# Diagonal and finest-level scores of the recurrence heads, taken as channel sums in rounded products

## The reference, cut to what matters

```
b = jnp.cumsum(gi, axis=-2)
diff = b[..., :, None, :] - b[..., None, :, :]
decay = jnp.exp(jnp.where(causal, diff, -jnp.inf))
scores = jnp.einsum('bhtk,bhsk,bhtsk->bhts', qi, ki, decay)
o = jnp.einsum('bhts,bhsv->bhtv', scores, vi) + ...
```

## Time and profile before

| what | value |
|---|---|
| median of 3 runs | 1628.47 us |
| the profiled execution, its own time | 1628.97 us |
| its span | 1627.2 us |
| PE busy | 1620.3 us, 100% |
| DVE busy | 1109.9 us, 68% |
| ACT busy | 842.2 us, 52% |
| POOL busy | 181.7 us, 11% |
| a stream slab, from issue to landing (median) | 4.7 us |

### The profile page before, as it was taken

How to read it: one execution, slowest core, us unless ns; L and a number is a source line. 1 busy time by engine, 2 the same in 40 slices (tenths; PEclk the granted TensorE clock), 3 DMA queues, 4 the chain that set the end, 5 groups by cost and what they waited for, 6 DMA issues and landing times.

```text
span 1627.2 us, 35049 instructions
## 1 busy us (share of the span) xinstructions
PE 1620.3 (100%) x13332; PEld 1615.8 (99%) x13332; DVE 1109.9 (68%) x1917; ACT 842.2 (52%) x1192; POOL 181.7 (11%) x166
## 2 busy tenths in 40 slices
PE   9999999999999999999999999999999999999999
PEld 9999999999999999999999999999999999999999
DVE  7548767888888876655986665566555665555774
ACT  7575765666666665433654334443444334443452
POOL 3101000111111100055300000000000000035200
PEclk9999999999999999999999999999999999999999
DMA  9577895565555467755675865588557775555564
GB/s 274 161 230 225 267 270 174 164 191 162 192 166 181 155 206 229 270 181 185 173 214 186 247 207 180 188 259 243 174 181 242 245 222 185 181 197 181 167 192 144
DMA packets 151178, 329.17 MB, mean 202 GB/s; under 512 B 16944, under 2 KB 79536, under 8 KB 150608
## 3 DMA queue, kind: packets, MB, share of 16 engines
q1 hardware_dynamic: 143888, 326.00, 64.3%
q10 hardware_dynamic: 7232, 2.43, 0.6%
HBM read 310.08 MB, written 18.30 MB: 202 GB/s over the span
## 4 chain that ended last, share of the span: by engine, by line
PE 98%; DMA 1%; DVE 1%; ACT 0%; SPq 0%; issue 0%
PE bank L380 29%; PE bank L381 29%; PE bank L382 28%; PE bank L398 3%; PE bank L400 3%; PE bank L403 2%; PE bank L768 1%; DMA raw<-in_stream 1%; PE bank L795 0%; PE bank L787 0%; PE bank L766 0%; PE bank L788 0%; PE bank L757 0%; PE bank L732 0%; PE bank L770 0%; PE bank L778 0%
## 5 line engine op out<-in xcount | busy, mean ns | idle before, releaser
L355 ACT CAST whi<-raw 128x1024 fp32r<-128x1024 f32 x532 | 547.9, 1048 | 470.7 <-PE bank L382 388.5
L380 PE MATMUL bank<-a_hi,whi 128*128 128x264 f32 x2576 | 734.2, 285 | 0.1
L381 PE MATMUL bank<-a_hi,wlo 128*128 128x264 f32 x2576 | 729.7, 283 | 0.0
L382 PE MATMUL bank<-a_lo,whi 128*128 128x264 f32 x2576 | 729.4, 283 | 0.0
L360 DVE TENSOR_TENSOR wlo<-raw,whi 128x1024 fp32r<-128x1024 f32 x518 | 629.6, 1246 | 109.8 <-ACT whi L355 108.8
L380 PEld LDWEIGHTS bank<-a_hi,whi 128*128 128x128 f32 x2576 | 485.2, 188 | 0.8 <-issue 0.7
L381 PEld LDWEIGHTS bank<-a_hi,wlo 128*128 128x128 f32 x2576 | 485.5, 188 | 0.1
L382 PEld LDWEIGHTS bank<-a_lo,whi 128*128 128x128 f32 x2576 | 482.9, 187 | 0.0
L380 PE MATMUL bank<-b_hi,whi 128*128 128x264 f32 x1280 | 363.1, 284 | 0.0
L381 PE MATMUL bank<-b_hi,wlo 128*128 128x264 f32 x1280 | 362.6, 283 | 0.0
L382 PE MATMUL bank<-b_lo,whi 128*128 128x264 f32 x1280 | 362.4, 283 | 0.0
(11 more groups left out here) (222 smaller groups left out, 1497.7 us busy)
## 6 DMA issues: line engine op xcount, KB each, us to landing
raw<-in_stream SPq DMA_DIRECT2D x532, 512.0 KB, 4.7
m_spill<-stage SPq DMA_DIRECT2D x32, 132.0 KB, 3.7
lev<-m_spill SPq DMA_DIRECT2D x16, 264.0 KB, 2.8
room<-in_x SPq DMA_DIRECT2D x7, 528.0 KB, 7.8
S<-in_state_hgrn SPq DMA_DIRECT2D x6, 512.0 KB, 6.7
out_new_hgrn_sample<-S SPq DMA_DIRECT2D x6, 512.0 KB, 6.8
S<-in_state_gla SPq DMA_DIRECT2D x5, 512.0 KB, 6.7
out_new_gla_sample<-S SPq DMA_DIRECT2D x5, 512.0 KB, 7.5
```

Of the source, the lines that this page charges most:

```text
L355: act.copy(whi[:, s, :], raw[:, s, :]).then_inc(hi_ready, 1)
L380: pe.matmul(out, whi[:, s, w], hi[:, k0 + k, :], start=start and k == 0, stop=False)
L381: pe.matmul(out, wlo[:, s, w], hi[:, k0 + k, :], start=False, stop=False)
L382: mm = pe.matmul(out, whi[:, s, w], lo[:, k0 + k, :], start=False, stop=stop and k == HT - 1)
```

## The change

- Queries times keys of each token (the diagonal) are multiplied channel by channel on POOL (`dots_of`), the two factors of level 7 on DVE (`dots`, columns 0 to 127). ACT rounds these 384 columns (`dots_hi`), DVE makes their rest (`dots_lo`), and PE sums them over the channels by two rounded products with `ones_r` (`sum_dots`), placed behind `turn_kd` and ahead of slab 5. The two diagonal products and the product of level 7 go.
- ACT makes `turned` ahead of `slab(6)` instead of behind it, then waits for the products and rounds them. DVE waits for that rounding behind `slab(4)`.
- DVE's `slab(6)` moves from ahead of the masking to behind the seven additions. Level 7 is masked by an instruction of its own (128 columns), and the second mask instruction has two levels instead of three.
- `ident` is loaded by three transfers of 128 x 128 in another order of blocks, and the order of the blocks in `pairs` turns with it; the constants' semaphore counts 8 instead of 6.

```diff
@@ -183,0 +184,3 @@
+    with nc.sbuf_tensor("dots", [P, 3 * P], F32) as dots, nc.sbuf_tensor("dots_hi", [P, 3 * P], F32R) as dots_hi, \
+         nc.sbuf_tensor("dots_lo", [P, 3 * P], F32R) as dots_lo:
+        pass
@@ -250 +253 @@
-        "act": ["v_tok_ready", "lev_exp", "kd_exp", "kd_tok_ready", "sq_ready", "sq_rounded",
+        "act": ["v_tok_ready", "lev_exp", "kd_exp", "kd_tok_ready", "sq_ready", "parts_rounded",
@@ -252 +255 @@
-        "dve": ["sq_parted", "lev_sub", "lev_ready", "kd_ready", "masked", "probs_ready", "sg_ls",
+        "dve": ["parts_ready", "lev_sub", "lev_ready", "kd_ready", "masked", "probs_ready", "sg_ls",
@@ -308,0 +312,12 @@
+    def dots_now(H, D):
+        return 2 * H + 2 if D == 1 else H + (HH + 2)
+    def first_now(H):
+        return 2 * H + 2
+    def second_now(H):
+        return 2 * H + 3
@@ -318,0 +334,5 @@
+    def turned_blocks(dots):
+        ap = dots[:, 2 * P:3 * P]
+        return bass.AP(ap.tensor, ap.offset, [list(ap.ap[0]), [-P, 2], [1, P]])
@@ -486,2 +506 @@
-        for dst, name in ((masks, "masks"), (ident, "ident"), (head_gain, "head_gain"),
-                          (gate_b, "gate_b")):
+        for dst, name in ((masks, "masks"), (head_gain, "head_gain"), (gate_b, "gate_b")):
@@ -488,0 +508,2 @@
+        for to, of in ((0, 0), (1, 2), (2, 1)):
+            sp.dma_start(ident[:, to * P:(to + 1) * P], t["ident"][:, of * P:(of + 1) * P]).then_inc(const_landed, 16)
@@ -701 +722 @@
-        pe.wait_ge(const_landed, 16 * 6)
+        pe.wait_ge(const_landed, 16 * 8)
@@ -762 +783 @@
-            pe.wait_ge(h_sem["lev_ready"], now(H))
+            pe.wait_ge(h_sem["lev_ready"], first_now(H))
@@ -764,4 +785 @@
-            for B in range(2):
-                at = slice(B * P, (B + 1) * P)
-                pe.matmul(DG[:, 2 * B * P:(2 * B + 1) * P], k_b[:, at], q_b[:, at], start=True, stop=True)
-            for l in range(1, LEVELS):
+            for l in range(1, LEVELS - 1):
@@ -770,2 +788,6 @@
-            pe.matmul(DG[:, P:2 * P], lev[:, 0, 1, :], lev[:, 0, 0, :], start=True, stop=True)\
-              .then_inc(h_sem["scores_done"], 1)
+            pe.matmul(DG[:, 3 * P:4 * P], lev[:, 0, 1, :], lev[:, 0, 0, :], start=True, stop=True)
+        def sum_dots(H, D):
+            pe.wait_ge(h_sem["parts_ready"], dots_now(H, D))
+            pe.matmul(DG[:, 0:3 * P], ones_r[:], dots_hi[:], start=True, stop=False)
+            pe.matmul(DG[:, 0:3 * P], ones_r[:], dots_lo[:], start=False, stop=True).then_inc(h_sem["scores_done"], 1)
@@ -787,2 +809,2 @@
-                pe.matmul(O[d][:, 0:2 * P], v_tok[:, 0, v], pairs[:, 0:2, :], start=True, stop=False, skip_group_check=True)
-                mm = pe.matmul(O[d][:, P:2 * P], v_tok[:, 1, v], pairs[:, 2, :], start=False, stop=True, skip_group_check=True)
+                pe.matmul(O[d][:, 0:2 * P], v_tok[:, 0, v], pairs[:, 1:3, :], start=True, stop=False, skip_group_check=True)
+                mm = pe.matmul(O[d][:, P:2 * P], v_tok[:, 1, v], pairs[:, 0, :], start=False, stop=True, skip_group_check=True)
@@ -800 +822 @@
-                pe.wait_ge(h_sem["sq_parted"], now(H))
+                pe.wait_ge(h_sem["parts_ready"], second_now(H))
@@ -824,0 +847 @@
+            sum_dots(H, D)
@@ -1139 +1161,0 @@
-            slab(6)
@@ -1140,0 +1163,4 @@
+            act.wait_ge(h_sem["kq_ready"], second_now(H))
+            act.wait_ge(h_sem["lev_ready"], second_now(H))
+            act.copy(dots_hi[:], dots[:]).then_inc(h_sem["parts_rounded"], 1)
+            slab(6)
@@ -1153 +1179 @@
-                act.copy(sq_hi[:], sq[:, 0, 0:NP_TOK]).then_inc(h_sem["sq_rounded"], 1)
+                act.copy(sq_hi[:], sq[:, 0, 0:NP_TOK]).then_inc(h_sem["parts_rounded"], 1)
@@ -1487 +1513 @@
-        dve.wait_ge(const_landed, 16 * 6)
+        dve.wait_ge(const_landed, 16 * 8)
@@ -1543,0 +1570,2 @@
+                if l == LEVELS - 1:
+                    return dve.tensor_tensor(lk, lk, lefts(k_b[:], h), ALU.mult)
@@ -1548 +1576 @@
-                dve.wait_ge(h_sem["kq_ready"], now(H))
+                dve.wait_ge(h_sem["kq_ready"], first_now(H))
@@ -1559,0 +1588,2 @@
+                dve.wait_ge(h_sem["lev_ready"], first_now(H))
+                dve.tensor_tensor(dots[:, 0:P], lev[:, LEVELS - 1, 0, :], lev[:, LEVELS - 1, 1, :], ALU.mult).then_inc(h_sem["lev_ready"], 1)
@@ -1571,0 +1602,2 @@
+            dve.wait_ge(h_sem["parts_rounded"], dots_now(H, D))
+            dve.tensor_tensor(dots_lo[:], dots[:], dots_hi[:].bitcast(F32), ALU.subtract).then_inc(h_sem["parts_ready"], 1)
@@ -1580 +1611 @@
-            for n, (first, last) in enumerate(((0, 4), (4, LEVELS - 1))):
+            for n, (first, last) in enumerate(((0, 4), (4, LEVELS - 2))):
@@ -1584 +1615,2 @@
-            dve.tensor_tensor(pairs[:], DG[:, 0:3 * P].rearrange("s (b t) -> s b t", b=3),
+            dve.tensor_tensor(probs[:, LEVELS - 2, :], DG[:, 0:P], both[:, LEVELS - 2, :], ALU.mult).then_inc(h_sem["masked"], 1)
+            dve.tensor_tensor(pairs[:], DG[:, P:4 * P].rearrange("s (b t) -> s b t", b=3),
@@ -1588 +1620 @@
-                to = cells(pairs[:, 0, :], h, h, 2 * P - h, 2 * h)
+                to = cells(pairs[:, 0, :], h, P + h, -(P + h), 2 * h)
@@ -1591 +1623 @@
-                dve.wait_ge(h_sem["masked"], (LEVELS + 1) * H + (l + 3))
+                dve.wait_ge(h_sem["masked"], (LEVELS + 2) * H + (l + 4))
@@ -1602,2 +1635,2 @@
-                dve.wait_ge(h_sem["sq_rounded"], now(H))
-                dve.tensor_tensor(sq_lo[:], sq[:, 0, 0:NP_TOK], sq_hi[:].bitcast(F32), ALU.subtract).then_inc(h_sem["sq_parted"], 1)
+                dve.wait_ge(h_sem["parts_rounded"], second_now(H))
+                dve.tensor_tensor(sq_lo[:], sq[:, 0, 0:NP_TOK], sq_hi[:].bitcast(F32), ALU.subtract).then_inc(h_sem["parts_ready"], 1)
@@ -1900 +1933 @@
-        pool.wait_ge(const_landed, 16 * 6)
+        pool.wait_ge(const_landed, 16 * 8)
@@ -1940,0 +1974,6 @@
+        def dots_of(H):
+            pool.wait_ge(h_sem["kq_ready"], first_now(H))
+            pool.tensor_tensor(turned_blocks(dots), q_b[:, 0:NP_TOK].rearrange("c (b t) -> c b t", b=2),
+                               k_b[:, 0:NP_TOK].rearrange("c (b t) -> c b t", b=2), ALU.mult).then_inc(h_sem["kq_ready"], 1)
@@ -1956,0 +1996,3 @@
+        pool.wait_ge(units_summed, HEADS)
+        with pool.Fori(0, 1) as H:
+            dots_of(H)
@@ -1962,0 +2007 @@
+            dots_of(H + 1)
```

More of the change, by code:

```diff
@@ L1138, in head @@
             slab(5)
+            turned(H, D)
+            act.wait_ge(h_sem["kq_ready"], second_now(H))
+            act.wait_ge(h_sem["lev_ready"], second_now(H))
+            act.copy(dots_hi[:], dots[:]).then_inc(h_sem["parts_rounded"], 1)
             slab(6)
-            turned(H, D)
             if D == 2:
```

## The result

The changed kernel takes **1631.63 us** (median of 20 runs, 1630.99 to 1633.79) beside 1628.55 us for the kernel before (20 runs, 1627.60 to 1629.47). The ratio is 1.0021, with a 95% interval of 1.0014 to 1.0027: 3.1 us slower. The interval lies clear of 1, and the difference just under the 3.3 us that were named as the bound of what a measurement can tell. The forecast was 1630.1, range 1626.0 to 1634.4: the median lies inside, 1.5 above the forecast. The profiled execution took 1631.36 us with a span of 1629.3, so its span is 2.1 us longer than the span before.

What follows compares the result with a forecast made beforehand. PE was taken to bound the kernel, with 98% of the chain. Head 0 (-0.32), head 1 (+0.53), heads 2 to 7 (+1.0) and 8 to 11 (+0.4) summed to +1.6: 1630.1 us on the median, range 1626.0 to 1634.4.

Steps and rivals of the forecast that it cites:

- PE alone: PE's products per head: six go (-0.67 us), two rounded ones come (0.35); without a wait 0.32 us gained (0.19 to 0.43).
- The new wait ahead of slab 5: PE waits for DVE's rest of the products before slab 5; in a head like head 2 nothing lost, nothing to spare.
- The wait for the squares: At the squares' sums DVE's rest comes at 11.76, seen 11.81; PE waits 0.39 us, so heads 2 to 7 lose 0.17 each.
- The restart of 0.10: At PE's squares' sums: starting again behind a wait costs about 0.10 us.
- DVE is in time: Rival, squares' rest: heads 0 to 7 keep 0.32 us each, heads 8 to 11 lose 0.4 in all; 1626.3 us, chance 0.17.
- no wait costs anything: Rival, all twelve heads: each gains 0.32 us, -3.9 in all, so 1624.6 us; chance 0.09.
- POOL holds DVE: Rival, DVE's additions: POOL's product delays them 0.58 us in heads 1 to 7, +4.1, so 1634.2 us; chance 0.22.
- Heads 8 to 11 have no rest of squares: Step for the last four heads: only the new sums ahead of slab 5 come later, 0.11 us each, +0.4 together.
- The sum: Total over the twelve heads: +1.6 us on the profiled execution, 1630.1 us on the median.

Runs made afterwards that it cites:

- e1: Changed kernel with the first half of DVE's level differences moved from ahead of the squares' rest to behind slab(8), all heads: 1627.17 us, ratio to before 0.9993.
- e5: e1 with PE's two rounded sums moved from ahead of slab 5 to behind its second block: 1624.89 us, ratio to before 0.9979.
- e2: Changed kernel with the level differences moved behind slab(8) in heads 0 to 7 alone: 1628.39 us, ratio to before 1.0001.
- e8: Changed kernel with POOL's product of queries and keys cut to one column per block in heads 1 to 11: 1633.13 us, ratio to before 1.0027.
- e4: Changed kernel with DVE's slab(6) put back ahead of the masking: 1633.54 us, ratio to before 1.0035.
- e3: Changed kernel with the level differences moved behind slab(8) in heads 8 to 11 alone: 1629.81 us, ratio to before 1.0011.

## Why the prediction was right, and where it was not

- **PE alone.** Held. Once nothing waits (e1), the squares' sums start 11.44 us after L778 instead of 11.74: a gain of 0.30 a head, forecast 0.32. The two sums take 0.26 + 0.18 us from start to start; the 0.08 above twice 0.18 is the change from full to rounded products. Before, slab 5's first product paid it (0.20 to the next start, 0.11 now), and in e5, where it is the first again, it pays 0.21. So the cost has moved and is about the same, as was said. The starts behind slab 5's first product, in the kernel before (325.22) and in the changed one (324.59):

```profile
325.42 0.28 PE L381 MATMUL bank<-a_hi,wlo 128*128 128x264 f32 x1
...
324.70 0.28 PE L401 MATMUL bank<-a_hi,wlo 128*128 128x264 f32 x1
```

- **The new wait ahead of slab 5.** PE lost nothing there in head 2, as said. But ACT was the later one: DVE waited 0.34 us for the rounding, because it had started `kd` earlier against PE than in the head I counted from (321.37 against L778 at 322.23: 0.86 ahead instead of 0.37). `dots_lo` started 1.23 us after L778 instead of 1.30. That the wrong engine cost so little is luck in part: the sum had ACT's rounding (1.28) only 0.02 ahead of DVE. In e1 DVE itself comes there at 1.25 to 1.31 in heads 2 to 6. Whether an earlier rounding on ACT would help by itself was not tried.
- **The wait for the squares.** This is the core of the forecast, and it held in place, sign and nearly in size: seven waits, in heads 1 to 7; in heads 2 to 7 `sq_lo` done 11.72 us after L778 (forecast 11.76); head 1 at +0.54 (forecast +0.53), heads 2 to 7 at +0.14 each (forecast +0.17). The restart of 0.10 is there as well (0.22 instead of 0.12 for the first sum). e1 and e2 show that it is this wait. The rival of "DVE is in time" is out by these rows, "no wait costs anything" with it; e5 (1624.89) comes near the time it named (1624.6) once these waits, POOL's and those at the new sums are out of the way.
- **POOL holds DVE.** The rival falls: e8 leaves heads 2 to 7 at 27.34 to 27.37 us. e4 shows that it was near: with a rest ahead of the masks, POOL and DVE do collide.
- **The failed step.** "Heads 8 to 11 have no rest of squares", and so I let nothing but the new sums wait there, +0.11 a head. But the squares' halves are added on POOL, and the row for it (0.91 us) stood among my own rows; I used it as a price for POOL's product and did not ask who waits for this instruction, nor what DVE does beside it. Measured: +2.0 us in heads 8 to 10, forecast +0.3; in e3, with POOL's wait gone, these three heads stand at +0.04. The Trainium skill's rule that I had cited ("SBUF — State Buffer", Who interferes with whom), that the two engines exclude each other, acts here the other way round: DVE holds POOL. The trace agrees with the exclusion (2.74 us instead of 0.74) and adds that POOL can stay out over several DVE instructions that follow without idle time; in heads 8 and 10 it got in at one of the steps between them (1.60). The trace of the kernel before had shown such a hold: in head 2 a copy of two columns on POOL lasted 2.16 us, until the two rests on DVE beside it were over (322.60 to 324.95); in the changed kernel the shortest of these copies took 0.19:

```profile
322.83 2.16 POOL L1934 COPY cum<-totals 128x2 f32 x1 [22.67 <-DVE kd L1559]
```

- **The sum.** +1.6 forecast, +2.1 in the span, +2.4 in the profiled executions' times, +3.1 in the medians. That the span comes so near the forecast is luck: heads 0 to 10 lost 3.1 us, twice their forecast of 1.5, with the whole excess in heads 8 to 10, and the opening (-0.65) and head 11 with the end (-0.31) hid a part of it. The profiled execution was one with a single long wait for POOL; two more had two, and lie at 1632.3 and 1632.5. What the opening adds or takes differs by up to 1.4 us between profiles, and why stays open.

## What to carry to other kernels

Work taken off the engine that sets the time is a gain only if the next thing it waits for is early enough: read the lead of each supplier at each meeting point (here 0.70 us for the squares' rest), and where work is added ahead of it, move work that nobody waits for (the next head's level differences) behind it. Ask this of every kind of iteration apart, since another kind may meet another supplier (POOL's addition). And put a short product that waits for a late operand between products that do not, a few blocks into the stream, instead of at its head.

## What the runs showed of the hardware that was not expected

- DVE instructions with two SBUF operands, issued without idle time, can keep a POOL addition out for their whole row: 0.74 us alone (e1), 2.74 us behind four level differences and a rest of 1.22 us. POOL's product beside DVE's masking from PSUM took its 0.74. If POOL gets in, the DVE instruction behind it is the one that is held (1.75 instead of 1.22). Which of the two happens differs between executions of one kernel (head 10: 1.60 once, 2.75 twice), about 1 us of the total each time.
- A rounded product of 384 columns costs 0.26 us straight behind full-precision products and 0.17 inside a run of rounded ones (e5), so the change of kind costs about 0.08 us in both of the places where these runs put it.
